# A two-block transformer kernel in fp32: the first gate and up weights of the feed-forward multiplied directly instead of through quarter sums

## The chip, the cores and the metric

The kernel runs on one core of a Trainium2 chip. The metric is device time in microseconds (us) of one execution. The core has a matrix engine (TensorE, PE in the profile), a vector engine (VectorE, DVE), an activation engine (ScalarE, ACT), GpSimd (POOL) and a queue for DMA issues (SyncE, SP). They run their own programs in order and wait for each other through semaphores. Matmul results land in PSUM, which has 8 banks of 512 fp32 columns.

## What is computed

Two transformer blocks over 512 tokens of width 1024. The first has two kinds of attention and a mixture of 64 experts; the second has retention and latent attention, and then the part that matters here:

```
h = h + rmsnorm(mix, post_mix_norm)
hn = rmsnorm(h, pre_ffn_norm)
ff = (silu(hn @ w_gate) * (hn @ w_up)) @ w_down        # D_FF = 2816
h = h + rmsnorm(ff, post_ffn_norm)
```

A gated embedding of each layer follows. All of it is fp32.

## The kernel before

**Three products for one.** A product of fp32 matrices in full precision is made from parts: each operand is split into a high part (rounded by a copy of ACT, `act_split`, `hi_until`) and a low part (operand minus high part, a subtraction on DVE, `dve_split`, `lo_until`), and `three` (L666 to L670) multiplies high by high, low by high and high by low into the same bank. A weight unit of 128 x 2048 elements is loaded by SP into one of three raw buffers (`whole`), turned into a high part in one of two buffers (`high`) and a low part (`low`). Before ACT writes the high part of unit k, `hi_until` calls `used(act, order[k - PARTS])`, which waits until PE has filled the last bank that unit k-2 feeds. From the first gate unit on, the high parts lie in buffers of their own (`late_hi`), the low parts in `late_lo`, the raw weights in `late_raw`.

**Gate and up by seven products.** The 22 units of gate and up (11 each, taken in turn: gate 0, up 0, gate 1, ...) are each a 1024 x 256 block of weights. It is cut into quarters A11, A12, A21, A22, the turned rows hn into quarters B11 to B22, and the product is made from seven products of quarters or of sums of quarters (Winograd's form of Strassen's method) instead of eight. For that GpSimd makes the sums S1 to S4 of each unit in place (`quarter_sums`, L2894 to L2902), ACT the high parts (`sums_hi`, L792), DVE the low parts (`sums_lo`, L799), and the results are added up again by DVE when they leave PSUM (`first_sums` to `last_sums`, L1643 to L1678). Each unit takes 7 x 4 x 3 = 84 matmuls of 256 columns. On the side of the rows the sums T1 to T4 are made once:

```
PRODUCTS = (("A11", "B11"), ("A12", "B21")), (("S1", "T1"), ("S2", "T2")), (("S4", "B22"), ("A22", "T4")), (("S3", "T3"),)
```

**The stretch before it.** The output projection of the mixer ("om", L668 to L670 with the tile omT) makes four tiles of 128 tokens, each in two banks, 12 matmuls of 512 columns for a bank: tile i goes to banks 2i (om0) and 2i+1 (om1), so that bank 6 is the last of unit om0 and bank 7 the last of om1. DVE then takes tile by tile: it adds the banks (L1584), multiplies by the gain (L1586), waits for ACT's sum of squares (L654) and its root (L658), adds the scaled rows to x (L1588), and, one tile later, scales x by the root of the next norm into `xn6` (L1577). PE turns the rows of xn6 by transposes into banks (L1314).

In the kernel before, GpSimd makes the quarter sums of three units and then the low parts of the first two in that stretch (L799 on POOL, four operations), and ACT makes their high parts between the norms (`between_norms`). The transposes go to banks so that one holds two chunks of half the tokens; the quarters are read straight from the banks, by ACT for high parts (L807) and for plain copies of the other half (L1895), by DVE for low parts (L1605) and differences (L1612). The first unit's products are queued in PE behind each of these in turn: B11, B21, T1, T2, B22, T4, T3. All of the queues' orders are written out by hand.

Behind gate and up comes w_down ("down"), whose left operands are the products ff in high and low parts.

Of the kernel before, what the change touches and what calls it, by code (L numbers as in the profile page):

```python
# [20 lines left out]
F32 = mybir.dt.float32  # L21
# [154 lines left out]
def build(nc, a, out):  # L176
    ctx = ExitStack()
    with ctx:
# [9 lines left out]
        def at(name, lo, shape, dt=F32):  # L188
# [28 lines left out]
        OPS = ("B11", "B21", "T1", "T2", "B22", "T4", "T3")  # L217
        OPS_AT = (8192, 16384, 10240, 38656, 40704, 42752, 44800)
        op_hi = {n: at(n + "h", F0 + lo, [4, Q], F32R) for n, lo in zip(OPS, OPS_AT)}
        op_lo, op_raw = [{n: at(n + k, F0 + lo + 1024, [4, Q], d) for n, lo in zip(OPS, OPS_AT)}  # L220
                         for k, d in (("l", F32R), ("r", F32))]
# [6 lines left out]

        copies, partial = at("copies", F0 + 35328, [2, Q]), at("partial", F0 + 35840, [3, Q])
        up_sum = at("up_sum", F0 + 36608, [4, Q])  # L230
# [165 lines left out]

        ff_units = [units_of[name][n] for n in range(n_ff) for name in ("gate", "up")]
        n_late = ff_units[0].n
        for m, u in enumerate(ff_units):
            u.sums = m  # L400
# [128 lines left out]
        plan("hT4", DC)  # L529

        for m, u in enumerate(ff_units):
            u.pairs = [bk.take(1, (J["hT4"][(4 * (m + 1) + k) % 8].bank,))[0] for k in range(4)]
            u.last = u.pairs[-1]
# [253 lines left out]
        def sums_hi(act, m, k):  # L787
            u = ff_units[m]
            act.wait_ge(S("w_sums"), m + 1)
            if m >= 2:  # L790
                full(act, ff_units[m - 2].last)
            act.activation(high(u, 7 * Q2)[:, SUM_PIECES[k]], whole(u, 7 * Q2)[:, SUM_PIECES[k]],  # L792
                           ACT.Copy).then_inc(S("sums_hi"), 1)

        def sums_lo(eng, m, k):
            u = ff_units[m]
# [368 lines left out]
        OP_ORDER = ("B11",) * 4 + ("B21",) * 4 + ("T1", "T2", "B22", "T4", "T3")  # L1165

        def op_ready(name, c):

            first = OP_ORDER.index(name) + 1
            return first + c if OP_ORDER.count(name) == 4 else first  # L1170

        def rows_half(c, h):

            job = J["hT4"][4 * h + c // 2]
            return banks[job.bank][:, Q * (c % 2):Q * (c % 2 + 1)], job
# [5 lines left out]
        def pe_second(pe):  # L1181
# [121 lines left out]
            def half_rows(j, i, c):  # L1303

                lo = Q * (c % 2) + P * (i % 2)
                return banks[J["hT4"][j].bank][:, lo:lo + P]

            for job in J["hT4"]:
                claim(pe, job)
            for i in range(NT):  # L1310
                pe.wait_ge(S("xn6"), i + 1)
                for c in range(DC):
                    j = 4 * (i // 2) + c // 2
                    mm = pe.transpose(half_rows(j, i, c), xn6(i)[:, P * c:P * (c + 1)], ident)  # L1314
                    if i % 2 and c % 2:
                        fill(mm, J["hT4"][j])
# [3 lines left out]
            for m, u in enumerate(ff_units):  # L1320
                his, los = quarters(high(u, 7 * Q2)), quarters(low(u, 7 * Q2))
                for k, job in enumerate(u.pairs):
# [4 lines left out]
                    for h, (left, right) in enumerate(PRODUCTS[k]):  # L1327
                        for c in range(4):
                            if m == 0:
                                pe.wait_ge(S("op_lo"), op_ready(right, c))  # L1330
                            mm = three(pe, banks[job.bank][:, Q * h:Q * (h + 1)], (his[left][:, c, :], los[left][:, c, :]),
                                       (op_hi[right][:, c, :], op_lo[right][:, c, :]), c == 0, c == 3)
# [134 lines left out]
        def dve_second(v, chain, evac):  # L1467
# [131 lines left out]
            def direct_lo(name, first):  # L1599
                for c in range(4):  # L1600
                    src, job = rows_half(first + c, 0)
                    full(v, job)

                    v.wait_ge(split_hi, hi_number["op", name, c | 1])
                    v.scalar_tensor_tensor(op_lo[name][:, c, :], src, PRM("pre_ffn", first + c),  # L1605
                                           op_hi[name][:, c, :].bitcast(F32), ALU.mult, ALU.subtract).then_inc(S("op_lo"), 1)

            def less(name, first, other, signal):

                for c in range(4):  # L1610
                    src, job = rows_half(first + c, 0)
                    ins = v.scalar_tensor_tensor(op_raw[name][:, c, :], src, PRM("pre_ffn", first + c), other[:, c, :],  # L1612
                                                 ALU.mult, ALU.subtract)
                    if c % 2:
                        free(ins, job)
                read(v, [job])
                v.sem_inc(S("op_sums"), 1)

            direct_lo("B11", 0)
            v.wait_ge(split_hi, hi_number["op", "b12"])  # L1620
            less("T1", 0, op_raw["T3"], 1)
            direct_lo("B21", 4)
            v.wait_ge(split_hi, hi_number["op", "b22"])
            chain(v.tensor_tensor(op_raw["T2"][:, :, :], op_raw["B22"][:, :, :], op_raw["T1"][:, :, :], ALU.add))
            v.sem_inc(S("op_sums"), 1)
            operand_lo("T1")
            less("T4", 4, op_raw["T2"], 3)
# [4 lines left out]
            operand_lo("T3")  # L1632

# [30 lines left out]
            def middle_sums(m):  # L1664
# [3 lines left out]
                if m:  # L1668
                    read(v, [ff_units[m - 1].pairs[3]])
# [1281 lines left out]
```

## Time and profile before

| what | value |
|---|---|
| median of 3 runs | 2074.44 us (2073.94 to 2077.29) |
| profiled execution, its own time | 2073.24 us |
| its span | 2071.4 us |
| busy in the span: PE, DVE, ACT, POOL | 86%, 44%, 36%, 15% |
| mean granted TensorE clock | 0.954 of full speed |

The span is what the profiler sees from the first to the last instruction; 1.8 us of the execution lie around it. Times below are us from the span's start. PE's clock has two levels, 1.2 and 2.4 GHz, shown as 0.5 and 1.0 of full speed. In a timeline a row's duration runs until its result is there; operations of one engine follow each other about 0.1 us before that.

### The profile page before, as it was taken

To read this page: it belongs to the slowest core of one execution; us is meant where nothing else is said; L and a number is where in the kernel's file an instruction comes from. 1 tells how busy PE (TensorE), PEld (TensorE's weight loads), DVE (VectorE), ACT (ScalarE), POOL (GpSimd) and SP (SyncE) were. 2 spreads that over 40 slices of the span, in tenths; PEclk is the share of its full clock that TensorE was granted. 3 is DMA by queue.
4 is the path that set the end of the run, shared out by engine and by line. 5 is a ranking of instruction groups with operands and counts; after the bars stand their busy time and mean duration, and the time that the engine had idled before them with its cause. 6 is when DMAs were issued, how large, how long until landed. Compare 5 with 4: busy or idle time off the path is not lost.

```text
span 2071.4 us, 37813 instructions
## 1 busy us (share of the span) xinstructions
PE 1772.4 (86%) x15166; PEld 1280.3 (62%) x15166; DVE 918.5 (44%) x1703; ACT 740.2 (36%) x1369; POOL 313.1 (15%) x298
## 2 busy tenths in 40 slices
PE   7999999787877787767777877789999599999988
PEld 5677788544444443434444444378767499998876
DVE  4455435532222222222222222365375878886245
ACT  4444522233222322232223222343465544444143
POOL 0000000000000000000000000640011668870020
PEclk9999999899999999999999999999999799999999
DMA  6222222699999999999999999843232033334212
GB/s 206 77 83 63 81 102 97 281 371 420 428 425 428 426 426 425 428 425 426 426 426 426 427 425 426 356 124 92 65 92 67 5 103 103 103 102 143 102 61 81
DMA packets 108338, 506.17 MB, mean 244 GB/s; under 512 B 9400, under 2 KB 58808, under 8 KB 74976
## 3 DMA queue, kind: packets, MB, share of 16 engines
q1 hardware_dynamic: 100144, 491.28, 59.4%
q10 hardware_dynamic: 6512, 9.73, 1.7%
q0 software_dynamic: 1600, 4.02, 0.7%
q8 instruction: 58, 0.95, 0.2%
q14 instruction: 24, 0.20, 0.0%
HBM read 497.32 MB, written 2.11 MB: 241 GB/s over the span
## 4 chain that ended last, share of the span: by engine, by line
PE 59%; DMA 29%; DVE 7%; issue 2%; ACT 2%; SPq 1%; POOL 0%; ACTq 0%; POOLq 0%; DVEq 0%
DMA ring<-in_w 27%; PE bank L668 13%; PE bank L669 12%; PE bank L670 12%; PE bank L2477 8%; PE bank L2389 4%; PE bank L2468 3%; PE bank L856 2%; PE bank L882 1%; PE bank L868 1%; DMA raw<-in_w_in 1%; SPq L2027 1%; PE bank L2486 1%; PE bank L1204 1%; DVE x L1588 0%
## 5 line engine op out<-in xcount | busy, mean ns | idle before, releaser
L2477 PE MATMUL bank<-ring,XTs 128*32 128x256 f32 x4032 | 284.8, 426 | 112.6 <-DMA ring<-in_w 109.7
L2730 DVE TENSOR_TENSOR x<-x,bank 128x512 f32<-128x512 f32 x264 | 163.9, 682 | 482.7 <-PE bank L2468 481.9
L2477 PEld LDWEIGHTS bank<-ring,XTs 128*32 128x32 f32 x4032 | 154.2, 120 | 245.0 <-issue 181.5
L2486 PE MATMUL bank<-ring,aT 128*32 128x256 f32 x2048 | 123.8, 381 | 90.0 <-DVE aT L2750 90.0
L2256 ACT ACTIVATE y<-bank 32x256 f32<-32x256 f32 x256 | 96.1, 376 | 225.1 <-PE bank L2468 139.0
L668 PE MATMUL bank<-hTh,w_hi 128*128 128x512 f32 x362 | 147.2, 407 | 5.5 <-DVE hTl L820 2.9
L2389 PE MATMUL bank<-arena,oh 128*32 128x256 f32 x2048 | 144.2, 421 | 4.4 <-DVE oh L2712 2.9
L772 DVE TENSOR_TENSOR w_lo<-raw,w_hi 128x2048 fp32r<-128x2048 f32 (+4 forms) x47 | 98.2, 2094 | 110.8 <-ACT w_hi L756 110.7
L2486 PEld LDWEIGHTS bank<-ring,aT 128*32 128x32 f32 x2048 | 66.7, 109 | 128.5 <-issue 96.2
L670 PE MATMUL bank<-hTl,w_hi 128*128 128x512 f32 x362 | 143.1, 395 | 0.0
L669 PE MATMUL bank<-hTh,w_lo 128*128 128x512 f32 x362 | 143.0, 395 | 0.0
L2836 POOL COPY sel<-side 128x8 f32 x62 | 11.9, 191 | 866.9 <-DVE og L2720 866.9
L2468 PE MATMUL bank<-y,g 64*128 64x512 f32 x528 | 131.4, 615 | 2.8 <-ACT y L2256 1.8
L2389 PEld LDWEIGHTS bank<-arena,oh 128*32 128x32 f32 x2048 | 90.1, 124 | 56.1 <-DVE oh L2712 18.3
L2225 ACT ACTIVATE xe<-bank 128x256 f32<-128x256 f32 x64 | 24.6, 384 | 276.1 <-PE bank L2389 276.1
L799 DVE TENSOR_TENSOR late_lo<-late_raw,late_hi 128x2048 fp32r<-128x2048 f32 (+1 forms) x40 | 95.7, 2393 | 17.6 <-ACT late_hi L792 17.6
L756 ACT ACTIVATE w_hi<-raw 128x2048 fp32r<-128x2048 f32 (+4 forms) x47 | 80.3, 1718 | 63.3 <-PE bank L670 61.7
L2228 ACT ACTIVATE XTs<-bank 128x256 f32<-128x256 f32 x64 | 24.7, 386 | 171.4 <-PE bank L2395 171.4
L668 PEld LDWEIGHTS bank<-hTh,w_hi 128*128 128x128 f32 x362 | 68.7, 190 | 27.1 <-issue 8.2
L2468 PEld LDWEIGHTS bank<-y,g 64*128 64x128 f32 x528 | 45.4, 186 | 61.9 <-issue 59.2
L2744 DVE COPY Hs<-bank 128x256 f32<-128x256 f32 x64 | 27.2, 425 | 125.0 <-PE bank L2477 125.0
L668 PE MATMUL bank<-w_hi,hTh 128*128 128x512 f32 (+2 forms) x232 | 80.2, 346 | 2.6 <-ACT arena L1831 2.2
(479 smaller groups left out, 3862.7 us busy)
## 6 DMA issues: line engine op xcount, KB each, us to landing
ring<-in_w SPq DMA_DIRECT2D x190, 2048.0 KB, 19.6
raw<-in_w_in SPq DMA_DIRECT2D x25, 1024.0 KB, 5.4
late_raw<-in_w_gate SPq DMA_DIRECT2D x11, 1024.0 KB, 5.4
late_raw<-in_w_up SPq DMA_DIRECT2D x11, 1024.0 KB, 5.4
late_raw<-in_w_down SPq DMA_DIRECT2D x11, 1024.0 KB, 5.0
raw<-in_w_out SPq DMA_DIRECT2D x4, 1024.0 KB, 5.0
third<-in_w SPq DMA_DIRECT2D x2, 2048.0 KB, 22.6
raw<-in_w_o SPq DMA_DIRECT2D x4, 1024.0 KB, 5.6
```

The costliest lines, as they stand in the source:

```text
L668: pe.matmul(dst, left[0], right[0], start=start, stop=False)
L669: pe.matmul(dst, left[1], right[0], start=False, stop=False)
L670: return pe.matmul(dst, left[0], right[1], start=False, stop=stop)
L756: ins = act.activation(hi, src, ACT.Copy)
L772: ins = v.tensor_tensor(lo, src, hi, ALU.subtract)
L799: eng.tensor_tensor(low(u, 7 * Q2)[:, cols], whole(u, 7 * Q2)[:, cols], high(u, 7 * Q2)[:, cols].bitcast(F32), ALU.subtract).then_inc(S("s ...
L2256: act.activation(y2[to:to + BLK, Q * (j % 2):Q * (j % 2 + 1)], Yb[BLK * j:BLK * (j + 1), :], ACT.Copy).then_inc(y_out, 1)
L2389: mm = pe.matmul(Xp[BLK * j:BLK * (j + 1), :], oh[u][:, t, :], h2[:, t, Q * j:Q * (j + 1)], start=(t == 0), stop=(t == NT - 1))
L2468: mm = pe.matmul(Sb[t % 2][n][:, :], g2[rows_, P * t:P * (t + 1)], y2[rows_, :], start=True, stop=True)
L2477: mm = pe.matmul(Hb[BLK * j:BLK * (j + 1), :], XTs[u][:, 4 * (c % 2) + 2 * h + c // 2, :], w[:, at_:at_ + Q], start=(h == 0 and c == 0), s ...
L2486: mm = pe.matmul(Yb[BLK * j:BLK * (j + 1), :], aT[:, r, h, :], ring[3 * u + 2][:, at_:at_ + Q], start=(h == 0 and r == 0), stop=(h == 1 an ...
L2730: ins = v.tensor_tensor(xs, xs, Sb[t % 2][n][:, :], ALU.add)
```

## The change

Gate 0 and up 0 no longer go through quarter sums: each is multiplied directly, two banks of 8 chunks x 3 = 24 matmuls of 512 columns, over the whole rows (high part `hTh`, low part `hT4l`). The list of units with quarter sums is now `sum_units`, the other 20. The transposes fill one bank per chunk with all 512 tokens. ACT copies each bank once to SBUF (`turned4`) with the gain of the norm, and makes the high part from that copy; DVE makes the low part from it as well. The quarters B11, B21 and B22 are read out of these; T1 to T4 are made by DVE from `turned4` behind the low parts. GpSimd only makes quarter sums, of the third unit on; the low parts of the sums are DVE's. ACT's high parts of gate 0 and up 0 are made by `hi_until`, that of gate 0 ahead of the norms' loop, that of up 0 behind the first root. DVE makes the low parts of gate 0 and up 0 (`lo_until`) behind the eight low parts of the rows. The core of the diff:

```diff
+        sum_units = ff_units[2:]
...
+        J["gate"], J["up"] = bk.take(2), bk.take(2)
+        for u, name in zip(ff_units, ("gate", "up")):
+            u.last = J[name][-1]
+
+        for u in sum_units:
+            u.pairs = bk.take(4)
...
         def sums_hi(act, m, k):
-            u = ff_units[m]
+            u = sum_units[m]
             act.wait_ge(S("w_sums"), m + 1)
-            if m >= 2:
-                full(act, ff_units[m - 2].last)
+            used(act, order[u.n - PARTS])
...
+            pe_to_feature(pe, J["hT4"], lambda i, c: xn6(i)[:, P * c:P * (c + 1)], lambda i: pe.wait_ge(S("xn6"), i + 1))
+            for name, u in zip(("gate", "up"), ff_units):
+                loaded(pe, u)
+                wh, wl = parts(u)
+                for job in J[name]:
+                    claim(pe, job)
+
+                for c in range(DC):
+                    if name == "gate":
+                        pe.wait_ge(S("op_lo"), c + 1)
+                    for k, job in enumerate(J[name]):
+                        cols = slice(P * k, P * (k + 1))
+                        mm = three(pe, banks[job.bank][:, :], (wh[:, c, cols], wl[:, c, cols]), (hTh[:, c, :], hT4l[:, c, :]),
+                                   c == 0, c == DC - 1)
...
+            for c in range(DC):
+                v.wait_ge(split_hi, hi_number["hT4", c])
+                v.tensor_tensor(halves_of(hT4l[:, c, :]), turned_chunk(c), halves_of(hTh[:, c, :].bitcast(F32)),
+                                ALU.subtract).then_inc(S("op_lo"), 1)
+            lo_until(v, ff_units[1].n)
+            v.wait_ge(S("op_lo"), DC)
+            b11, b12, b21, b22 = op_raw["T1"], op_raw["T3"], op_raw["T4"], op_raw["T2"]
+            for dst, one, other, op in ((b11, b11, b12, ALU.subtract), (b12, b22, b12, ALU.subtract), (b22, b22, b11, ALU.add),
+                                        (b21, b21, b22, ALU.subtract)):
+                chain(v.tensor_tensor(dst[:, :, :], one[:, :, :], other[:, :, :], op))
                 v.sem_inc(S("op_sums"), 1)
...
             operand_lo("T1")
             operand_lo("T2")
-            v.wait_ge(S("op_third"), 1)
-            operand_lo("B22")
+            sums_lo(v, 0, 0)
+            sums_lo(v, 0, 1)
             operand_lo("T4")
             operand_lo("T3")
+            for f, job in enumerate(J["up"]):
+                full(v, job)
+                v.wait_ge(S("silu_there"), f + 1)
+                ins = v.tensor_tensor(ff(f), ff(f), banks[job.bank][:, :], ALU.mult)
...
-            between_norms = (lambda: (sums_hi(act, 0, 0), sums_hi(act, 0, 1)), lambda: sums_hi(act, 1, 0),
-                             lambda: sums_hi(act, 1, 1), lambda: None)
+            hi_until(act, ff_units[0].n)
             for i in range(NT):
                 read(act, [J["om0"][i], J["om1"][i]])
                 n5.act(act, i, mixo[:, i, :], xn6(i), ssq, rstd)
                 if i:
                     act.wait_ge(S("x3"), i)
                     n6.act(act, i - 1, x[:, i - 1, :], xn6(i - 1), ssq2, rstd2)
-                between_norms[i]()
+                else:
+                    hi_until(act, ff_units[1].n)
...
+            for c, job in enumerate(J["hT4"]):
+                full(act, job)
+                free(act.activation(turned_chunk(c), halves_of(banks[job.bank][:, :]), ACT.Copy, scale=PRM("pre_ffn", c)), job)
+                if c:
+                    turned_hi(c - 1)
+            turned_hi(DC - 1)
...
-            for m in range(3):
-                quarter_sums(m)
-            for m in range(2):
-                for k in range(2):
-                    sums_lo(pool, m, k)
...
+            act.wait_ge(S("ff"), FC)
             for f in range(2, FC):
                 product_hi(f)
```

**Where instructions moved.** ACT's queue at the norms before, from the issue of the gain's load. `filledN` is the semaphore by which PE says that bank N is full, `arrivedN` says that a load has landed, `freedN` that a bank was read; L654 is the sum of squares, L658 the root:

```order
L2095 DMA gain_mix<-in_post_mix_norm 128x1024 [waits freed5,freed4]
L654 ACTIVATE xn6s,small<-arena 128x1024 [waits freed1,freed0]
L658 ACT_TABLE_LOAD
L658 ACTIVATE small<-small 128x1 [waits tile_means]
L792 ACTIVATE late_hi<-late_raw 128x2048 [waits w_sums]
L792 ACTIVATE late_hi<-late_raw 128x1536 [waits w_sums]
L654 ACTIVATE xn6s,small<-arena 128x1024 [waits freed3,freed2]
```

The same place in the changed kernel, whose line numbers are some 7 higher (L763 is `hi_until`, L661 the squares, L665 the root):

```order
L2089 DMA gain_mix<-in_post_mix_norm 128x1024 [waits freed5,freed4]
L763 ACTIVATE late_hi<-late_raw 128x2048 [waits filled6,arrived2]
L661 ACTIVATE xn6s,small<-arena 128x1024 [waits freed1,freed0]
L665 ACT_TABLE_LOAD
L665 ACTIVATE small<-small 128x1 [waits tile_means]
L763 ACTIVATE late_hi<-late_raw 128x2048 [waits filled7,arrived0]
L661 ACTIVATE xn6s,small<-arena 128x1024 [waits freed3,freed2]
```

The high part of gate 0 now stands ahead of the first sum of squares and waits for bank 6; that of up 0 stands behind the first root and waits for bank 7.

DVE's queue in the changed kernel, from the last xn6 (L1588 there) to the low parts of the first unit with sums (L805):

```order
L1588 TENSOR_SCALAR xn6s<-x,small 128x1024 [waits dve_own]
L1612 TENSOR_TENSOR hT4l<-turned_75,hTh 128x512 [waits split_hi] x4
L1612 TENSOR_TENSOR hT4l<-turned_76,hTh 128x512 [waits split_hi] x4
L779 TENSOR_TENSOR late_lo<-late_raw,late_hi 128x2048 [waits hi_made] x2
L1619 TENSOR_TENSOR turned_75<-turned_75 128x1024 [waits op_lo]
L1619 TENSOR_TENSOR turned_75<-turned_76,turned_75 128x1024 [waits dve_own]
L1619 TENSOR_TENSOR turned_76<-turned_76,turned_75 128x1024 [waits dve_own]
L1619 TENSOR_TENSOR turned_76<-turned_76 128x1024 [waits dve_own]
L1607 TENSOR_TENSOR T1l<-turned_75,T1h 128x1024 [waits dve_own,split_hi]
L1607 TENSOR_TENSOR T2l<-turned_76,T2h 128x1024 [waits split_hi]
L805 TENSOR_TENSOR late_lo<-late_raw,late_hi 128x2048 [waits sums_hi]
```

The low part of gate 0, which PE's first direct product waits for (`loaded`), stands behind all eight low parts of the rows; the quarter sums of the rows stand behind both.

## Rows read from the trace of the kernel before

**Rows 1.** Page, the chain that ended last, shares by engine.
```profile
PE 59%; DMA 29%; DVE 7%; issue 2%; ACT 2%; SPq 1%; POOL 0%; ACTq 0%; POOLq 0%; DVEq 0%
```
**Rows 2.** Windows: length; busy PE, PEld, DVE, ACT, POOL; clock, DMA share, GB/s.
```profile
1602.90:1618.70 15.80, 15.80 (x68) 12.34 (x66) 13.72 (x18) 10.61 (x14) 15.41 (x10) 1.00 0.22 72
1618.70:1642.40 23.70, 5.00 (x24) 4.62 (x24) 21.92 (x20) 8.34 (x19) 19.94 (x5) 0.58 0.00 0
...
1644.40:1662.30 17.90, 13.41 (x87) 12.73 (x86) 15.79 (x23) 11.00 (x19) 2.37 (x1) 0.84 0.00 1
1662.30:1874.30 212.00, 211.80 (x1765) 211.60 (x1764) 177.05 (x231) 91.07 (x107) 163.48 (x76) 1.00 0.33 105
```
**Rows 3.** Timeline of PE: start, duration, operation, idle before and its releaser.
```profile
1615.52 0.39 PE L670 MATMUL bank<-w_lo,omT 128*128 128x512 f32 x1
1641.06 3.67 PE L1314 MATMUL bank<-cst,xn6s 128*128 128x128 f32 x16 [6.08 <-DVE xn6s L1577]
1644.43 0.55 PE L668 MATMUL bank<-B11h,late_hi 128*128 128x256 f32 x1
1662.29 0.28 PE L668 MATMUL bank<-B11h,late_hi 128*128 128x256 f32 x1
1874.43 0.40 PE L668 MATMUL bank<-late_hi,ffh 128*128 128x512 f32 x1
1874.66 0.40 PE L669 MATMUL bank<-late_hi,ffl 128*128 128x512 f32 x1
```
**Rows 4.** Timeline of DVE in the norms.
```profile
1602.96 1.28 DVE L1584 TENSOR_TENSOR arena<-mix_scaled,bank 128x512 f32<-128x512 f32 x2 [4.17 <-DMA gain_mix<-in_post_mix_norm]
1607.24 2.23 DVE L1588 SCALAR_TENSOR_TENSOR x<-mix_scaled,small,x 128x1024 f32<-128x1024 f32 x1
1621.27 4.79 DVE L1588 SCALAR_TENSOR_TENSOR x<-mix_scaled,small,x 128x1024 f32<-128x1024 f32 x1
1631.19 4.16 DVE L1586 TENSOR_TENSOR mix_scaled<-arena,gain_mix 128x1024 f32<-128x1024 f32 x1
1636.01 3.71 DVE L1588 SCALAR_TENSOR_TENSOR x<-mix_scaled,small,x 128x1024 f32<-128x1024 f32 x1
1640.25 0.75 DVE L1577 TENSOR_SCALAR xn6s<-x,small 128x1024 f32<-128x1024 f32 x1
1641.71 0.75 DVE L1577 TENSOR_SCALAR xn6s<-x,small 128x1024 f32<-128x1024 f32 x1
```
**Rows 5.** Timeline of POOL there.
```profile
1604.73 2.27 POOL L2899 TENSOR_TENSOR late_raw<-late_raw 128x512 f32<-128x512 f32 x1
1619.48 19.16 POOL L799 TENSOR_TENSOR late_lo<-late_raw,late_hi 128x2048 fp32r<-128x2048 f32 x4
```
**Rows 6.** Timeline of ACT at the first norm.
```profile
1604.34 1.06 ACT L654 ACTIVATE xn6s<-arena 128x1024 f32<-128x1024 f32 x1 [7.88 <-DVE arena L1584]
```
**Rows 7.** Groups by form: count, busy us, mean ns, idle before.
```profile
L1741 DVE SCALAR_TENSOR_TENSOR e_tok<-e_tok,small,gain_ple 128x1024 f32<-128x1024 f32 x4 | 4.9, 1278 | 0.0
L1596 DVE TENSOR_TENSOR T4l<-T4r,T4h 128x1024 fp32r<-128x1024 f32 x1 | 1.2, 1219 | 0.0
L756 ACT ACTIVATE late_hi<-late_raw 128x2048 fp32r<-128x2048 f32 x16 | 30.6, 1914 | 95.8 <-PE bank L670 95.8
L807 ACT ACTIVATE hTh<-bank,small 128x512 fp32r<-128x512 f32 x8 | 4.7, 703 | 0.7 <-PE bank L636 0.7
L772 DVE TENSOR_TENSOR late_lo<-late_raw,late_hi 128x2048 fp32r<-128x2048 f32 x16 | 36.6, 2291 | 81.2 <-ACT late_hi L756 81.2
```
**Rows 8.** Timeline of ACT and of DVE behind gate and up.
```profile
1876.53 4.79 ACT L807 ACTIVATE ffh<-ffr 128x512 fp32r<-128x512 f32 x9
...
1878.87 12.13 DVE L819 TENSOR_TENSOR ffl<-ffr,ffh 128x512 fp32r<-128x512 f32 x20
```
**Rows 9.** Windows after PE idled until 1653.31: same columns as rows 2.
```profile
1655.00:1656.50 1.50, 1.48 (x7) 1.19 (x6) 1.50 (x2) 1.50 (x2) 0.00 (x0) 0.50 0.00 0
1656.50:1657.00 0.50, 0.50 (x4) 0.50 (x4) 0.50 (x1) 0.50 (x2) 0.00 (x0) 0.71 0.00 0
```

More of the change, by code:

```diff
@@ L1163, in build, with turned_chunk, halves_of @@
         NX = 2 * NBLK
[L1165 to L1175, printed above, removed]
+        OP_ORDER = ("T1", "T2", "T4", "T3")
+        def turned_chunk(c):
+            return turned4[c // 4][:, :, c % 4, :]
+        def halves_of(t):
+            return t.rearrange("p (h n) -> p h n", h=2)
         def sums_of(job):
@@ L1302, in pe_second, with operand @@
                     fill(mm, job)
[L1303 to L1311, printed above, removed]
-                for c in range(DC):
[L1313 to L1316, printed above, removed]
+            pe_to_feature(pe, J["hT4"], lambda i, c: xn6(i)[:, P * c:P * (c + 1)], lambda i: pe.wait_ge(S("xn6"), i + 1))
[4 more added lines that the diff above has]
+                    claim(pe, job)
+                for c in range(DC):
+                    if name == "gate":
[4 more added lines that the diff above has]
+                                   c == 0, c == DC - 1)
+                        if c == DC - 1:
+                            fill(mm, job)
+            def operand(name, c):
+                if name in op_hi:
+                    return op_hi[name][:, c, :], op_lo[name][:, c, :]
+                first, cols = dict(B11=(0, slice(0, Q)), B21=(4, slice(0, Q)), B22=(4, slice(Q, T)))[name]
+                return hTh[:, first + c, cols], hT4l[:, first + c, cols]
             PRODUCTS = (("A11", "B11"), ("A12", "B21")), (("S1", "T1"), ("S2", "T2")), (("S4", "B22"), ("A22", "T4")), (("S3", "T3"),)
-            for m, u in enumerate(ff_units):
+            for m, u in enumerate(sum_units):
                 his, los = quarters(high(u, 7 * Q2)), quarters(low(u, 7 * Q2))
@@ L1608, in less @@
[L1608 to L1616, printed above, removed]
-                v.sem_inc(S("op_sums"), 1)
-            direct_lo("B11", 0)
@@ L1668, in middle_sums @@
                 if m:
-                    read(v, [ff_units[m - 1].pairs[3]])
-                chain(v.tensor_tensor(u2, copies[:, m % 2, :], sixth, ALU.add))
+                    read(v, [sum_units[m - 1].pairs[3]])
+                chain(v.tensor_tensor(u2, copies[m % 2], sixth, ALU.add))
                 free(v.tensor_tensor(u4, u2, fifth, ALU.subtract), job)
             def second_sums(m):
-                job = ff_units[m].pairs[2]
-                read(v, ff_units[m].pairs[1:2])
+                job = sum_units[m].pairs[2]
+                read(v, sum_units[m].pairs[1:2])
                 full(v, job)
@@ L1916, in product_hi @@
                 act_split(act, ("ff", f), ff_hi(f), ff(f))
-            direct_hi("B11", 0)
-            other_half("b12", op_raw["T3"], 0)
-            direct_hi("B21", 4)
-            other_half("b22", op_raw["B22"], 4)
-            operand_hi("T1", 1)
-            operand_hi("B22", 1)
-            operand_hi("T2", 2)
-            operand_hi("T4", 3)
-            act.wait_ge(S("op_third"), 1)
-            operand_hi("T3", 3)
-            for m, u in enumerate(ff_units):
-                n, ready = m // 2, 1 <= m < len(ff_units) - 1
+            for f, job in enumerate(J["gate"]):
+                full(act, job)
+                free(act.activation(ff(f), banks[job.bank][:, :], ACT.Silu), job)
+                read(act, [job])
+                act.sem_inc(S("silu_there"), 1)
+            operand_hi("T1", 1)
+            operand_hi("T2", 3)
+            sums_hi(act, 0, 0)
+            sums_hi(act, 0, 1)
+            operand_hi("T4", 4)
+            operand_hi("T3", 2)
+            for m, u in enumerate(sum_units):
+                n, ready = m // 2 + 1, m < len(sum_units) - 1
                 if m % 2:
                     for k in (2, 3):
-                        gated(n, k, ff_units[m - 1].pairs[3])
+                        gated(n, k, sum_units[m - 1].pairs[3])
                 full(act, u.pairs[0])
-                act.activation(copies[:, m % 2, :], sums_of(u.pairs[0])[0], ACT.Copy).then_inc(S("copied"), 1)
+                act.activation(copies[m % 2], sums_of(u.pairs[0])[0], ACT.Copy).then_inc(S("copied"), 1)
                 if ready:
```

103 lines of the change are left out of this document (37 added, 66 removed).

## The prediction

> **What bounds the kernel now.** I read the page's chain first: 59% of the span is PE and 29% DMA [rows 1]. The DMA share is the experts' weights, which the change leaves alone. It works between the mixer's output projection and w_down, so I cut that stretch into windows. The reader is to see four things. Until 1618.7 PE is fully busy with the projection [rows 2]. From 1618.7 to 1642.4 PE is busy for 5.0 of 23.7 us while DVE is busy for 21.9: the norms on DVE are the bound. The first unit of gate and up, 1644.43 to 1662.29, takes 17.9 us, with PE busy for 13.4 and its clock at 0.84. The other 21 units take 212.1 us, 10.10 each, with PE never idle [rows 2, 3]. So what counts is the moment at which w_down's first matmul starts, 1874.43. What comes later moves as a whole.
>
> The norms are slow for a reason. DVE's scaled add L1588 takes 4.79 and 3.71 us for two tiles and the multiply L1586 takes 4.16 [rows 4], where the same forms elsewhere take 1.28 and 1.22 [rows 7]. GpSimd works for 19.2 us without a break beside them [rows 5], and once it has stopped the xn6 operations take 0.75.
>
> **1. The norms.** The first tile's adds wait for the gain's load and end at 1604.2; ACT's squares start at 1604.34 [rows 4, 6]. In the change ACT's queue has the high part of gate 0 ahead of these squares, and it waits for bank 6, the last bank of om0. PE's last matmul into that bank starts at 1615.52 and ends at 1615.9 [rows 3]. The copy takes 1.9 us [rows 7], 1.8 until the next can start, so the squares start at about 1617.8, 13.5 us late. All of DVE's norm chain is queued behind the first root. PE is not: its four tiles have banks of their own. From squares to L1588 the rows give 1607.24 - 1604.34 = 2.90 us, a table load among it [rows 4, 6], so L1588 of the first tile starts at 1620.7. The copy for up 0 behind the first root hides beside DVE: bank 7 is full at 1618.7, and ACT is free again at 1622.3, before the next adds end at 1623.3.
>
> From there on GpSimd is silent. It still has the sums of the third unit, whose load is over by 1606.4 (a DMA share of 0.22 in 15.8 us [rows 2]); four operations of at most the 2.27 of [rows 5] are over by 1615.5, while DVE waits anyway. So DVE runs at its own pace: L1588 1.28, L1586 1.22, adds 1.28, xn6 0.75 [rows 4, 7], 0.6 for the small operations and ACT's root ahead of each scaling (1640.25 + 1.46 = 1641.71 is one xn6 and its preparation). The second tile follows after 1.28 + 1.28 + 1.22 + 0.62 = 4.4, the third and fourth after 4.4 + 0.61 + 0.75 = 5.76 each, and from the last L1588 to the end of the last xn6 it is 1.28 + 2.74 = 4.0 (2.74 from 1639.72, the end of L1588, to 1642.46). Sum 19.9: the last xn6 ends at 1640.7, against 1642.46 now. **Gain 1.8.** Nearly all that the quiet GpSimd gives back is spent on the wait for bank 6.
>
> **2. From the last xn6 to the first product.** Now 1644.43 - 1642.46 = 2.0 us. In the change PE turns the third tile's eight chunks from 1639.2 on and the fourth's behind them, at 0.23 each [rows 3]; the first bank is full, and ACT starts, at 1641.35. ACT then has 16 operations: eight scaled copies out of banks, 4.7 us from the first start to the last end [rows 7], and eight high parts, 8/9 of 4.79 [rows 8]; together 9.0. DVE keeps up (0.61 each [rows 8]) and ends the eighth low part 0.7 later. Only then comes the low part of gate 0, 2.29 [rows 7], for which PE waits. With 0.2 for hand-overs PE starts at 1653.5, 12.8 us behind the last xn6. **Loss 10.8.** PE's waits chunk by chunk hide nothing, since the weights' low part comes last.
>
> The Trainium skill says (ScalarE: Activation LUTs, What ACT_TABLE_LOAD costs) that a per-partition pointer operand costs an activation about 93 ns; by its figure the copies would follow each other every 0.61 us and the sum would be 0.2 us higher. The rows' eight copies with such a scale decide, and I keep their 4.7.
>
> **3. The first two units.** Now 1644.43 to 1662.29 and 10.10 more: 28.0 us. In the change 2 x 48 = 96 matmuls of 512 columns at 0.23 [rows 3] make 22.1. The clock is at half when PE starts, as it was after the idle time before 1653.31, and there it took until about 1656.7, 3.4 us, to come back (0.71 in the half microsecond from 1656.5 [rows 9]); that loses half of 3.4. Sum 23.8. **Gain 4.2.** Had PE gone on with seven products it would be 20.2; the two extra eighths cost less than the first unit's waits for B21, T1 and T2 that they remove.
>
> **4. What hides behind them.** PE needs T1, T2 and the third unit's parts at 1653.5 + 23.8 = 1677.3. DVE makes the second low part and the four sums of quarters by 1661 (2.3 + 4 x 1.25). ACT is in PE's way here: its two silus wait for gate's banks, full at 1666.2, so that T1's high part starts at 1667.4, T2's ends at 1669.5, the third unit's two pieces at 1671.3 and 1672.7. DVE's low parts follow at 1673.6 to 1674.6 and 1676.6, 3 us and 4 us ahead of their need (the second piece is wanted at 1680.2). GpSimd's next sums run from about 1671.6, since their load starts when gate's banks are full. Cost 0. Cover gone, it is the rival below.
>
> **5. The rest.** 20 units at 10.10 make 202.0. ACT's new wait for all products ahead of w_down's high parts costs at most the 2 us until DVE's last one; PE has 11 us of w_down's first part to do meanwhile. 0.
>
> **Sum.** -1.8 + 10.8 - 4.2 = +4.8: w_down starts at 1653.5 + 23.8 + 202.0 = 1879.3 instead of 1874.43. The profiled execution took 2073.24 and would take 2078.1; its median is 1.2 higher, which gives 2079.2. I say **2079**, slower by 0.2%. About 0.2%, 4.1 us, is what a measurement of this kernel can tell from no change, and I am close to it.
>
> **Rivals.**
> *The wait for bank 6 costs nothing (faster).* It would have to be over by 1602.4, so that the copy is done when the squares are due: if bank 6 counted as full by an earlier use. The queue's row names bank 6, and PE fills it for om0 only at 1615.9; against it. Then L1588 starts at 1607.24 as now, the chain runs its 19.9, about 1 more for the sums of the third unit beside the first tile, and the last xn6 ends at 1628.2, 14.2 earlier: 2079.2 - 12.4 = 2066.8. Chance 0.07.
> *GpSimd is not what stretches DVE.* Then the chain from the first L1588 keeps its 35.2 us instead of 19.9, and the time is 2094.5. The return to 0.75 when GpSimd stops speaks against. 0.03.
> *The first unit with sums waits.* DVE's two low parts, T4, T3 and the two multiplies of up have GpSimd beside them. If they stretch as L1588 does, the next unit's low part, wanted at 1687.4, comes 1 to 3 us late: 2080.2 to 2082.2. By the Trainium skill (SBUF — State Buffer, Who interferes with whom) a DVE operation with two SBUF inputs and a GpSimd one that reads SBUF exclude each other for a whole instruction; four sums of 1.3 would then add at most 5.2 to that queue, which is within this rival. The steady units, which hold as many of both and never make PE wait [rows 2], speak against. 0.15.
> *The start is shorter than worked out.* ACT and DVE hand over faster, the clock comes up during the transposes, or the loop of norms overlaps more: 1 to 3 us less, 2076 to 2078. 0.15.
> *The change doesn't do what it says* holds in part: GpSimd does work between the norms, on one unit, but DVE waits then; it is in the forecast.
>
> **How the numbers follow.** Forecast 0.60, 2077 to 2081.5. Slower by over 0.2% is above 2078.6: 0.42 of the forecast's 0.60, with 0.15 and 0.03, 0.60. Within 0.2%: 0.18 + 0.15 = 0.33. Faster: 0.07. The range of 8 in 10 takes in the two small rivals beside the forecast, with 2 us for the estimates added up: 2074.5 to 2083.5.
>
> **What would show it.** Right: ACT idle until about 1616 ahead of the high part of gate 0; L1588 at 1.28 for all four tiles; PE idle for about 10 us behind the transposes, released by DVE's low part of gate 0; first direct product near 1653.5; 20 units of 10.1. Wrong: ACT's squares near 1604, L1588 still above 3 us, or PE waiting behind up 0.

## The result, and the profile after

The changed kernel takes 2079.02 us (median of 20 runs, 2075.02 to 2086.2), the kernel before on the same chip 2074.55 (20 runs, 2071.45 to 2079.13): a ratio of 1.0021, 95% interval 1.0013 to 1.0029. It is slower by 0.2%, as forecast, to 0.02 us of the forecast time. So close a hit says little: the 20 runs lie 11 us apart, and the interval of the ratio alone is 3.3 us wide. Whether the terms are right is read below.

The page's shares of the changed kernel, beside [rows 1]:

```profile
span 2077.9 us, 37612 instructions
...
PE 59%; DMA 29%; DVE 6%; ACT 2%; issue 2%; SPq 1%; POOL 1%; ACTq 0%; POOLq 0%; DVEq 0%
```

The shares cannot show a change of this size. The stretch cut into windows by stage does, as in [rows 2]; columns: length, then busy time and count of PE, weight loads, DVE, ACT and GpSimd, PE's granted clock, DMA share, GB/s:

```profile
1602.90:1615.90 13.00, 13.00 (x58) 10.46 (x57) 2.51 (x3) 0.00 (x0) 5.12 (x4) 1.00 0.54 180
1615.90:1640.40 24.50, 8.27 (x37) 6.78 (x36) 14.73 (x27) 13.39 (x22) 0.00 (x0) 0.70 0.00 0
1640.40:1653.50 13.10, 5.20 (x24) 4.40 (x22) 7.35 (x14) 10.51 (x22) 0.00 (x0) 0.63 0.00 0
1653.50:1677.30 23.80, 20.49 (x84) 16.82 (x85) 15.84 (x12) 9.78 (x10) 2.26 (x1) 0.86 0.14 45
1677.30:1879.00 201.70, 201.37 (x1664) 200.46 (x1663) 171.78 (x215) 86.39 (x102) 162.36 (x76) 1.00 0.34 105
```

In the first window ACT does nothing and DVE 2.51 us of work in 13: both wait, DVE for the gain's load until 1606.39 and then for ACT. GpSimd's four operations all fall into that wait. In the last window PE is full again.

DVE's timeline in the norms of the changed kernel, the answer to [rows 4]; columns: start, duration, engine, line, operation, out<-in, count, and the idle time before with what ended it:

```profile
1606.39 1.28 DVE L1595 TENSOR_TENSOR arena<-mix_scaled,bank 128x512 f32<-128x512 f32 x2 [4.25 <-DMA gain_mix<-in_post_mix_norm]
1607.78 1.23 DVE L1597 TENSOR_TENSOR mix_scaled<-arena,gain_mix 128x1024 f32<-128x1024 f32 x1
1622.41 0.15 DVE L669 TENSOR_SCALAR small<-small 128x1 f32<-128x1 f32 x1 [13.40 <-ACT xn6s L661]
1623.85 0.16 DVE L671 RECIPROCAL small<-small 128x1 f32<-128x1 f32 x1 [1.29 <-ACT small L665]
1624.05 1.28 DVE L1599 SCALAR_TENSOR_TENSOR x<-mix_scaled,small,x 128x1024 f32<-128x1024 f32 x1
...
1643.29 0.75 DVE L1588 TENSOR_SCALAR xn6s<-x,small 128x1024 f32<-128x1024 f32 x1
```

All four scaled adds, as a group (count, then busy us and mean ns):

```profile
L1599 DVE SCALAR_TENSOR_TENSOR x<-mix_scaled,small,x 128x1024 f32<-128x1024 f32 x4 | 5.1, 1285 | 0.1
```

ACT's timeline, the answer to [rows 6]:

```profile
1619.35 1.92 ACT L763 ACTIVATE late_hi<-late_raw 128x2048 fp32r<-128x2048 f32 x1 [19.54 <-PE bank L677]
1621.17 1.04 ACT L661 ACTIVATE xn6s<-arena 128x1024 f32<-128x1024 f32 x1
```

And PE's timeline, the answer to [rows 3]:

```profile
1642.64 3.68 PE L643 MATMUL bank<-cst,xn6s 128*128 128x128 f32 x16 [0.71 <-DVE xn6s L1588]
1656.81 0.79 PE L675 MATMUL bank<-hTh,late_hi 128*128 128x512 f32 x1 [10.49 <-DVE late_lo L779]
1657.40 0.63 PE L676 MATMUL bank<-hTh,late_lo 128*128 128x512 f32 x1
...
1882.61 0.40 PE L675 MATMUL bank<-late_hi,ffh 128*128 128x512 f32 x1
```

The wait for bank 6 ends ACT's 19.54 us of idle time ahead of gate 0's high part (with the copy behind it, ACT's squares start 13.4 us later behind the adds than in experiment 1), and the queue's end is the 10.49 us for which PE waits on DVE's low part of gate 0. PE starts on the units and finds its clock at half (0.63 us a matmul instead of 0.39).

**One shift to take out first.** The norms' first adds start at 1606.39, in the kernel before at 1602.96 [rows 4]: 3.4 us late before any changed instruction. Two windows of both executions tell why; first the kernel before, then the changed one:

```profile
1500.00:1530.00 30.00, 26.57 (x122) 19.75 (x114) 27.80 (x37) 20.78 (x31) 8.99 (x18) 1.00 0.46 124
1530.00:1560.00 30.00, 28.74 (x167) 21.02 (x167) 17.69 (x63) 17.98 (x55) 0.00 (x0) 1.00 0.11 36
```

```profile
1500.00:1530.00 30.00, 27.60 (x119) 20.18 (x118) 26.31 (x35) 20.01 (x31) 8.99 (x18) 0.95 0.47 125
1530.00:1560.00 30.00, 27.70 (x146) 19.97 (x146) 17.07 (x55) 16.93 (x46) 0.00 (x0) 0.94 0.11 37
```

The granted clock was 0.95 and 0.94 there instead of 1.00, and 5% and 6% of 30 us are 3.3 us. It goes with the execution and not with the change: in the first experiment's, whose code there is the same, the clock is 1.00 in both windows and the adds start at 1602.68, while experiments 2 and 5 again had 0.94 in both and start them at 1605.46 and 1605.32. The clock is not all of it: experiment 3 had 1.00 in both windows and its adds start at 1606.01, for a reason that lies further ahead and was not looked into. On the other side, PE's last stretch from w_down's first matmul to the end of the span took 197.0 us before and 195.3 after; over the nine profiled executions it was 195.3 twice, 197.0 five times, 199.7 and 199.8, and went with the kernel's content in no way that I can see. So traces are compared below by four marks, counted from the first adds: that takes both shifts out.

| kernel | adds to the end of the last xn6 | to the first product | to w_down's first matmul | adds to w_down | median us, ratio |
|---|---|---|---|---|---|
| before | 39.50 | 1.97 | 230.00 | 271.47 | 2074.55, 1 |
| the change | 37.65 | 12.77 | 225.80 | 276.22 | 2079.02, 1.0021 |
| 1. no wait for bank 6 | 26.31 | 12.37 | 225.83 | 264.51 | 2069.07, 0.9971 |
| 2. low part first | 37.77 | 3.47 | 225.23 | 266.47 | 2069.62, 0.9970 |
| 3. both | 26.24 | 3.47 | 225.69 | 255.40 | 2059.44, 0.9918 |
| 4. before, its low parts on DVE | 28.19 | 4.41 | 228.78 | 261.38 | 2064.18, 0.9946 |
| 5. as 3, GpSimd busy | 34.64 | 3.08 | 224.09 | 261.81 | 2067.58, 0.9950 |
| 6. as 3, sums after the norms | 24.26 | 4.03 | 225.05 | 253.34 | 2058.41, 0.9916 |
| 7. as 3, GpSimd copies | 28.72 | 3.08 | 225.86 | 257.66 | 2060.47, 0.9927 |

Each mark is a start read from a timeline; the end of the last xn6 is its start and 0.75. The ratios are against runs of the kernel before made beside each kernel (medians 2074.13 for experiments 1 to 4 and 2075.12 for 5 to 7). They are not the quotients of the medians and differ from these by up to 0.0014, 3 us; the intervals given below are wider than that. The change adds 4.75 us between the adds and w_down.

### The profile page after: what moved, and what is told of

The parts are those of the page before. It is cut to its first block, busy times and chain, and to the rows that moved or that the text cites. A ratio compares the mean times of both kernels' runs of the same rounds, so it can differ in the third digit from the quotient of the medians.

```text
span 2077.9 us, 37612 instructions
## 1 busy us (share of the span) xinstructions
PE 1771.9 (85%) x15094; PEld 1274.1 (61%) x15094; DVE 902.7 (43%) x1683; ACT 737.9 (36%) x1362; POOL 278.6 (13%) x285
## 4 chain that ended last, share of the span: by engine, by line
PE 59%; DMA 29%; DVE 6%; ACT 2%; issue 2%; SPq 1%; POOL 1%; ACTq 0%; POOLq 0%; DVEq 0%
DMA ring<-in_w 27%; PE bank L675 13%; PE bank L676 12%; PE bank L677 12%; PE bank L2471 8%; PE bank L2383 4%; PE bank L2462 3%; PE bank L862 2%; PE bank L888 1%; PE bank L874 1%; DMA raw<-in_w_in 1%; SPq L2021 1%; PE bank L2480 1%; DVE w_lo L779 1%; PE bank L1207 1%
## 5 line engine op out<-in xcount | busy, mean ns | idle before, releaser
L805 DVE TENSOR_TENSOR late_lo<-late_raw,late_hi 128x2048 fp32r<-128x2048 f32 (+1 forms) x40 | 97.0, 2427 | 15.8 <-ACT late_hi L798 15.8
L763 ACT ACTIVATE w_hi<-raw 128x2048 fp32r<-128x2048 f32 (+4 forms) x47 | 80.3, 1718 | 64.1 <-PE bank L677 62.6
L675 PE MATMUL bank<-hTh,late_hi 128*128 128x256 f32 (+1 forms) x272 | 81.4, 299 | 10.8 <-DVE late_lo L779 10.5
```

Of the source, the lines that this page charges most:

```text
L675: pe.matmul(dst, left[0], right[0], start=start, stop=False)
L763: ins = act.activation(hi, src, ACT.Copy)
L805: eng.tensor_tensor(low(u, 7 * Q2)[:, cols], whole(u, 7 * Q2)[:, cols], high(u, 7 * Q2)[:, cols].bitcast(F32), ALU.subtract).then_inc(S("s ...
```

## Experiments

My theory was the forecast's: the change quiets GpSimd and that is worth 12 to 14 us, but it puts ACT's first squares behind a wait for bank 6 (13.5 us) and the low part of gate 0 behind eight low parts of rows (10 us). The rivals: GpSimd is not what stretches DVE, and the wait or the queue order costs nothing because something else is late too. Experiments 1 and 2 take one price each away.

### 1. Gate 0's and up 0's high parts without the wait

Line 760, in the function that makes high parts on ACT. Nobody reads the buffers of these two units' high parts before, so the wait that was taken from the general case can go:

```diff
-                if k >= PARTS:
+                if k >= PARTS and u.late not in (0, 1):
```

> The changed kernel, but ACT's high parts of gate 0 and up 0 do not wait for om's last banks (their buffers are not the ones that om reads). My theory: that wait holds all four norms back by 13.5 us, so the first L1588 (L1599 there) starts about 4.3 us behind the first adds, the last xn6 ends 12.4 us earlier against the adds, and the time falls by 12.4 us against the changed kernel, to about 2066.6 (before: 2074.5). Rival 1, the banks' wait is hidden by something else that is late too (the gain's load, PE's transposes): no change, 2079. Rival 2, GpSimd's sums of the third unit now meet the norms and stretch DVE again: 2070 to 2074.

Measured: 2069.07 us (12 runs), ratio 0.9971, interval 0.9959 to 0.9983. DVE's timeline, with the gap behind the first L1597 gone:

```profile
1602.68 1.28 DVE L1595 TENSOR_TENSOR arena<-mix_scaled,bank 128x512 f32<-128x512 f32 x2 [4.08 <-DMA gain_mix<-in_post_mix_norm]
1604.07 1.23 DVE L1597 TENSOR_TENSOR mix_scaled<-arena,gain_mix 128x1024 f32<-128x1024 f32 x1
...
1606.95 2.08 DVE L1599 SCALAR_TENSOR_TENSOR x<-mix_scaled,small,x 128x1024 f32<-128x1024 f32 x1
1608.95 1.27 DVE L1595 TENSOR_TENSOR arena<-mix_scaled,bank 128x512 f32<-128x512 f32 x2
1610.33 2.19 DVE L1597 TENSOR_TENSOR mix_scaled<-arena,gain_mix 128x1024 f32<-128x1024 f32 x1
```

The wait for bank 6 is real and it is the whole delay: without it the scaled add comes 4.3 us behind the adds, and adds to xn6 falls by 11.3. From adds to w_down it is 11.7, between the medians 10.0: the median lies just below the 2070 to 2074 of rival 2, and that rival holds in part. I had expected 13.5 less 1 us for GpSimd's sums of the third unit; those sums now run beside the first two tiles and cost 2 (experiment 6). PE still waits 11.2 us for the low part of gate 0.

### 2. The low part of gate 0 ahead of the rows' low parts

One line in DVE's order, ahead of the loop over the eight chunks:

```diff
+            lo_until(v, ff_units[0].n)
             for c in range(DC):
                 v.wait_ge(split_hi, hi_number["hT4", c])
```

> The changed kernel, but DVE makes the low part of gate 0 ahead of the eight low parts of the rows instead of behind them, in the 2.6 us in which it waits for ACT's first high part. My theory: PE's first direct product starts with the first chunk, about 3.4 us behind the start of ACT's copies instead of 12, and goes on at half clock and then as ACT delivers a chunk each 1.09 us; it needs 12.7 us for gate, so gate ends about 9.4 us earlier: 2069.6. Rival 1, only the 2.3 us of the low part itself are won: 2076.7. Rival 2, PE starts earlier but the third unit's parts become late, since ACT makes them behind the silus: between the two.

Measured: 2069.62 us (12 runs), ratio 0.9970, interval 0.9957 to 0.9983. DVE and then PE:

```profile
1643.15 2.28 DVE L779 TENSOR_TENSOR late_lo<-late_raw,late_hi 128x2048 fp32r<-128x2048 f32 x1
1645.86 0.69 DVE L1613 TENSOR_TENSOR hT4l<-turned,hTh 128x512 fp32r<-128x512 f32 x1 [0.43 <-ACT hTh L813]
```

```profile
1646.70 0.47 PE L675 MATMUL bank<-hTh,late_hi 128*128 128x512 f32 x1 [1.20 <-DVE hT4l L1613]
```

The low part lies where DVE waited for ACT's first high part anyway, and PE starts 3.47 us behind the last xn6 instead of 12.77. It then takes the chunks as they come, each 1.10 apart while six matmuls (two banks) take 1.4 at full clock, so it never waits for one. Of the 9.75 us between the adds and w_down 9.30 are the earlier start. My expectation had half clock here too; in this execution the clock was full from the first product on, so the first two units took 21.85 us and no longer 23.36, and most of that was lost again in the other 20, which took 203.38 and not 202.44.

### 3. Both

> Both edits together (no wait for om's last banks, low part of gate 0 first). My theory: the two are in series on the path and add up: -12.4 and -9.4 give about 2057.2 against 2079.0, and 17 us less than before the change. Rival: one hides the other, and the time is that of the better one alone, 2066 to 2070.

Measured: 2059.44 us (6 runs), ratio 0.9918, interval 0.9897 to 0.9938. Between adds and w_down the two edits give 11.71 and 9.75 alone and 20.82 together, 0.64 less than the sum: the two prices lie one after the other on the path and all but add up. The median is 2.2 us above the expected 2057.2. **This kernel is faster than both, by 0.8% than the one before** (0.7% by the medians).

### 4. The kernel before, with GpSimd's four low parts on DVE

Nothing else of the change. The two calls for unit 0 go behind the last xn6 on DVE, the two for unit 1 behind the rows' first low parts, and GpSimd's are taken out:

```diff
+            sums_lo(v, 0, 0)
+            sums_lo(v, 0, 1)
...
+            sums_lo(v, 1, 0)
+            sums_lo(v, 1, 1)
...
-            for m in range(2):
-                for k in range(2):
-                    sums_lo(pool, m, k)
```

> The kernel before, but the low parts of the first two units' sums are made by DVE (unit 0 behind the last xn6, unit 1 behind T3), and GpSimd makes quarter sums alone. This is the quiet GpSimd by itself, with nothing else of the change. My theory: GpSimd's 19.2 us stretched DVE's operations; without them the last xn6 ends about 12.4 us earlier, PE's first product starts 4 us later behind it, net -8.4: 2066.1. Rival, GpSimd's work is not what stretched DVE: the norms stay as long and the time rises by the 4 us, to 2078.5.

Measured: 2064.18 us (6 runs), ratio 0.9946, interval 0.9927 to 0.9965, 2 us better than expected. DVE's timeline, to be held against 2.23, 4.79 and 3.71 for L1588 in [rows 4]:

```profile
1608.07 2.33 DVE L1588 SCALAR_TENSOR_TENSOR x<-mix_scaled,small,x 128x1024 f32<-128x1024 f32 x1
...
1614.67 1.58 DVE L1588 SCALAR_TENSOR_TENSOR x<-mix_scaled,small,x 128x1024 f32<-128x1024 f32 x1
...
1622.20 1.28 DVE L1588 SCALAR_TENSOR_TENSOR x<-mix_scaled,small,x 128x1024 f32<-128x1024 f32 x1
...
1627.95 1.29 DVE L1588 SCALAR_TENSOR_TENSOR x<-mix_scaled,small,x 128x1024 f32<-128x1024 f32 x1
1631.90 3.95 DVE L799 TENSOR_TENSOR late_lo<-late_raw,late_hi 128x2048 fp32r<-128x2048 f32 x2
```

The norms shorten by 11.3 us and the low parts, 19.16 on GpSimd [rows 5], cost DVE 3.95 for unit 0. The first product comes 2.4 us later behind the last xn6 (4 expected), and the stretch from there to w_down is 1.2 shorter. GpSimd still makes the sums of three units here, so the first tiles keep some of their length (2.33 and 1.58). So GpSimd without its low parts was worth some 10 us to the kernel before by itself, and the rest of the change, as it was made, cost 15. With both edits the rest of the change is a gain: experiment 3 is 6.0 us shorter than this kernel from adds to w_down, 2.0 in the norms, 0.9 up to the first product and 3.1 behind it.

### 5 and 7. GpSimd's load put back

Is it GpSimd at all, or something that went with it? The kernel of experiment 3 gets four operations on GpSimd ahead of the third unit's sums; they read that unit's raw weights and write an area that nothing reads, so nothing of the computation changes. In 5 they are subtractions (two inputs), in 7 copies (one):

```diff
+            u = sum_units[0]
+            pool.wait_ge(arrived[u.n % RAW], u.loads)
+            for k in range(4):
+                n = (UNIT, 7 * Q2 - UNIT)[k % 2]
+                chain(pool.tensor_tensor(idle_area[:, 0:n], whole(u, n), whole(u, n), ALU.subtract))
```

In 7 the last line is `chain(pool.tensor_copy(idle_area[:, 0:n], whole(u, n)))`.

> The kernel of the third experiment (no wait for bank 6, low part of gate 0 first; 2059.4 us) with GpSimd's work put back beside the norms: four subtractions of 2048 and 1536 columns from the third unit's raw weights into an idle area, which nothing reads, ahead of the sums of its quarters. They take about as long as the four low parts did in the kernel before (19.2 us). Theory (GpSimd's reads and writes are what stretches DVE's operations of the norms): DVE's L1599, L1597 and xn6 go from 1.3-2.3 us to 2-5 us, the last xn6 comes 8 to 14 us later behind the first adds, and the time is 2059.4 + 11 = 2070 (2067 to 2074). Rival (what stretched DVE in the kernel before was its other data, the late_lo and late_hi area or ACT's high parts at the same time): DVE keeps its 1.3-2.3, time 2059 to 2062. Second rival (only the instruction count of GpSimd matters, and the sums of the quarters come too late for the third unit): PE waits behind up 0 and not before gate 0.

> As the kernel with GpSimd's work put back, but with four copies (one input) of the same columns instead of four subtractions (two inputs). Theory A (any GpSimd operation on SBUF stretches DVE's): DVE's operations of the norms that run beside a copy take 2 us and more, and the time lies above 2059.4 by about as much as GpSimd is busy longer, in the ratio of the subtractions' run. Theory B (it takes GpSimd's two inputs from SBUF): DVE keeps 1.2 to 1.3 beside the copies, and only the sums of quarters stretch it: 2059 to 2061.

Measured: 5 takes 2067.58 us (6 runs), ratio 0.9950, interval 0.9933 to 0.9968; 7 takes 2060.47 us (6 runs), ratio 0.9927, interval 0.9910 to 0.9944. GpSimd's timeline of 5, then of 7:

```profile
1609.26 15.52 POOL L2904 TENSOR_TENSOR idle_area<-late_raw 128x2048 f32<-128x2048 f32 x4 [81.08 <-DMA late_raw<-in_w_gate]
```

```profile
1605.89 9.67 POOL L2904 COPY idle_area<-late_raw 128x2048 f32<-128x2048 f32 x4 [77.97 <-DMA late_raw<-in_w_gate]
```

DVE's groups in the norms (busy us and mean ns after the bar), 5 and then 7:

```profile
L1600 DVE SCALAR_TENSOR_TENSOR x<-mix_scaled,small,x 128x1024 f32<-128x1024 f32 x4 | 11.1, 2767 | 0.1
L1598 DVE TENSOR_TENSOR mix_scaled<-arena,gain_mix 128x1024 f32<-128x1024 f32 x4 | 7.1, 1772 | 0.4
L1589 DVE TENSOR_SCALAR xn6s<-x,small 128x1024 f32<-128x1024 f32 x4 | 5.3, 1316 | 0.1
L1596 DVE TENSOR_TENSOR arena<-mix_scaled,bank 128x512 f32<-128x512 f32 x8 | 5.1, 676 | 4.2 <-DMA gain_mix<-in_post_mix_norm 4.2
```

```profile
L1600 DVE SCALAR_TENSOR_TENSOR x<-mix_scaled,small,x 128x1024 f32<-128x1024 f32 x4 | 7.6, 1889 | 0.1
L1598 DVE TENSOR_TENSOR mix_scaled<-arena,gain_mix 128x1024 f32<-128x1024 f32 x4 | 6.0, 1492 | 0.4
```

The theory stands: the work alone brings the stretched operations back. With nothing beside them (experiment 6) the norms take 24.26 us; 22.7 us of subtractions and sums make them 34.64, and 16.9 us of copies and sums 28.72. Take off the 1.98 that the sums cost in experiment 3 (as if they cost the same here), and 15.52 us of subtractions cost about 8.4 and 9.67 us of copies about 2.5. So theory B of experiment 7 is wrong, a copy stretches DVE's operation too (L1600 took 2.55 and 2.17 us beside them), but it costs 0.26 us for each of its microseconds where a subtraction costs 0.54.

That a copy costs less need not have to do with its one input. Single instructions of GpSimd, each beside the DVE operation that it met, from the timelines of both engines, first in 5:

```profile
1609.26 3.60 POOL L2904 TENSOR_TENSOR idle_area<-late_raw 128x2048 f32<-128x2048 f32 x1 [81.08 <-DMA late_raw<-in_w_gate]
1609.60 4.34 DVE L1600 SCALAR_TENSOR_TENSOR x<-mix_scaled,small,x 128x1024 f32<-128x1024 f32 x1
```

and then in 7:

```profile
1605.89 1.91 POOL L2904 COPY idle_area<-late_raw 128x2048 f32<-128x2048 f32 x1 [77.97 <-DMA late_raw<-in_w_gate]
1606.32 2.55 DVE L1600 SCALAR_TENSOR_TENSOR x<-mix_scaled,small,x 128x1024 f32<-128x1024 f32 x1
...
1610.17 1.23 DVE L1598 TENSOR_TENSOR mix_scaled<-arena,gain_mix 128x1024 f32<-128x1024 f32 x1
1610.26 2.90 POOL L2904 COPY idle_area<-late_raw 128x2048 f32<-128x2048 f32 x1
```

The subtraction ends at 1612.86 and DVE's add, begun inside it, 1.08 us later; the copy ends at 1607.80 and the add begun inside it 1.07 later. In the third pair DVE began 0.09 us first: it kept its 1.23, and the copy took 2.90 instead of 1.91. The long operations of the kernel before do the same: 4.79, 4.16 and 3.71 all end 1.08 or 1.09 us behind the end of one of GpSimd's low parts (1624.97, 1634.27, 1638.64). So both kinds of instruction hold DVE up in the same way, until they are over, and the copy is over sooner (1.91 us for 2048 columns against 3.60). Instructions of one length with one and with two inputs were not compared, so that the inputs count for nothing beyond this is not shown.

In time, 7 cannot be told from 3; the reading rests on the trace. Experiment 5 lost 6.6 us against 3 by the ratios, 8.1 by the medians and 6.4 from adds to w_down; PE had its full clock when gate 0 started, which gave back 1.6 (last section).

### 6. GpSimd's sums held back until the norms are over

```diff
+            pool.wait_ge(S("xn6"), NT)
             for m in range(len(sum_units)):
                 quarter_sums(m)
```

> The kernel of the third experiment with GpSimd's sums of quarters held back until the last xn6 is written, so that GpSimd does nothing at all between the norms. Theory (the 2 us by which the first two experiments' norms fell short of the chain worked out at 19.9 us from the first scaled add are these four sums beside DVE): L1597 and L1599 of the first two tiles go back to 1.22-1.28, the last xn6 comes 2 us earlier behind the first adds, and the time is 2057.4 (2056.4 to 2058.4), since the sums are needed only some 10 us later, when PE has two units of 22 us to do. Rival (the sums, now beside DVE's low parts of the rows and of up 0, stretch those instead): the first product comes no earlier, 2059 to 2061.

Measured: 2058.41 us (6 runs), ratio 0.9916, interval 0.9897 to 0.9936. Its groups of DVE in the norms:

```profile
L1599 DVE SCALAR_TENSOR_TENSOR x<-mix_scaled,small,x 128x1024 f32<-128x1024 f32 x4 | 5.1, 1285 | 0.1
...
L1597 DVE TENSOR_TENSOR mix_scaled<-arena,gain_mix 128x1024 f32<-128x1024 f32 x4 | 4.9, 1226 | 0.4
```

The norms lose their last 1.98 us, as the theory said, and 0.56 is lost again between the last xn6 and the first product (the rival's half: the sums now stretch DVE's low part of the first chunk to 1.64 us from 0.69, and the first GpSimd sum itself takes 3.24 us instead of 1.29). The ratio is that of experiment 3, so whether the rest, 1.4 us, shows in the time stays open.

## Why the prediction was right

**The norms.** Forecast 37.7 from adds to the last xn6 (1640.7 - 1602.96), measured 37.65. L1588 of before is L1599 of after, and all four take 1.28. The chain that I worked out for an undisturbed DVE, 4.3 and 19.9 us, is what experiment 6 runs: 24.26. Gain forecast 1.8, measured 1.85.

**From the last xn6 to the first product.** Forecast 12.8, measured 12.77: ACT starts 0.82 us behind the last xn6 (0.65 worked out), 16 operations of ACT from 1644.86 to 1653.74 are 8.9 (9.0 worked out), and the low part of gate 0 is the release of PE. The copies out of banks with a scale per partition:

```profile
1644.86 1.27 ACT L1889 ACTIVATE turned<-bank,prm 128x512 f32<-128x512 f32 x2 [1.80 <-PE bank L643]
...
1652.55 1.19 ACT L813 ACTIVATE hTh<-turned 128x512 fp32r<-128x512 f32 x2
```

A copy and a high part take 1.09 together in the steady part. An estimate by the Trainium skill's figure (ScalarE: Activation LUTs, What ACT_TABLE_LOAD costs) would have been 0.2 us higher; by the trace it came out at the rows'.

**The first two units.** Forecast 23.8, measured 23.36: first product 1656.81, first unit with sums 1680.17. PE's matmuls take 0.63 us until 1659.5 and 0.39 from 1659.96 on, so the clock came back after 3.1 us and not 3.4; the forecast was 0.44 too long, and this is 0.15 of it; 0.2 more is that the 96 matmuls follow each other at a little less than the rounded 0.23 (21.85 us for all of them at full clock in experiment 2). From the first product to w_down it is 225.80 against 230.00, a gain of 4.20 for 4.2 forecast, but two misses of 0.4 cancel in it: the first two units went from 27.94 to 23.36, a gain of 4.58, and the other 20, forecast to stay as they were, from 202.06 to 202.44. Experiment 3 against 4 gives 3.1 for the same two units: with the low parts off GpSimd the first unit of the kernel before takes 16.6 us and no longer 17.9. Its waits gave that: 4.5 us of them before and 2.5 in experiment 4, while the clock took 0.7 back (0.84 granted before, 0.69 there).

**What hides.** Right in its result. DVE's T4 and T3 took 2.31 and 2.32 us beside GpSimd instead of 1.22, held up as the Trainium skill's rule said (SBUF — State Buffer, Who interferes with whom), but PE never waited for the third unit: from 1603 to 1885 only two of its waits are over 1 us, the transposes' and gate 0's, and its wait for a low part of the sums is 0.2 in all. The rival of a first unit that waits did not happen.

**The rivals.** The wait that costs nothing: against it the 19.54 us on ACT, and experiment 1. GpSimd is not the cause: against it experiments 4, 5 and 6. The time a rival gave was good too: 2066.8 for a kernel without the wait, 2069.07 measured. 1 of the missing 2.3 us is that the third unit's sums cost 2 and not the 1 allowed; the rest was not traced.

**What was lucky.** The three stretches and their sum agree within 0.1 us each, but the median of runs mixes stretches that vary (3.4 us ahead of the norms, 195.3 to 199.8 behind w_down's start). An execution could have come out 3 us off with every step right. The term for the clock was lucky too: the forecast took 1.7 us from one row of the kernel before, the change lost about 1.6, and the same products lost between nothing and 2.4 in the experiments (last section). That two misses of 0.4 cancel behind the first product is luck as well.

## To carry to other kernels

A change that quiets an engine is paid out only where that engine's victim is the bound, and only if the same edit does not put a new wait at the head of the victim's queue: write down, for each queue, what now stands ahead of the first instruction on the path, and what that waits for. Here the norms gained 13.3 us by the quiet GpSimd and lost 11.4 by the wait, the first product came 10.8 later behind them (9.3 by the order of one queue), and the direct units gave back 4.2: a loss of 4.7 us, 0.2%, which two lines turned into a win of 0.8%. A general rule's wait (every high part waits for the last user of its buffer) is worth a look where a unit moves to a place in which nobody reads the buffer before.

## What the runs showed of the hardware

- GpSimd and DVE hold each other up for the rest of an instruction (experiments 5 and 7): beside GpSimd's subtractions DVE's scaled add takes 3.7 to 4.8 us for 1.28 and the multiply 2.4 to 4.2 for 1.22 (the kernel before and experiment 5), beside copies the scaled add takes 2.2 to 2.6, and the multiply, which began just ahead of one, its 1.23. DVE's xn6, which reads one tensor from SBUF, is held up as well: 2.62 and 1.34 for 0.75. Adds with one input from a bank never stretched: 676 to 682 ns in experiments 3, 5, 6 and 7 and in the change, GpSimd busy or not. The other way round, GpSimd's sum of 512 columns takes 1.29 us alone, often 2.15 beside DVE, and up to 3.4 (experiment 2).
- The clock at which the first products run changed from execution to execution, and I can't tell what sets it: PE's granted clock was half for the first 3.1 us in the change, for 3.6 us in experiment 3 and for 5.1 us in experiment 1 (0.63 us a matmul), while in experiments 2 and 5 the first product took 0.47 and the next 0.39 to 0.40 at once. In 6 and 7 it started full and fell to half for 3.4 us in the middle of gate 0, as PE's timeline of experiment 6 has it:

```profile
1632.27 0.39 PE L677 MATMUL bank<-hT4l,late_hi 128*128 128x512 f32 x1
1632.50 0.54 PE L675 MATMUL bank<-hTh,late_hi 128*128 128x512 f32 x1
1632.83 0.63 PE L676 MATMUL bank<-hTh,late_lo 128*128 128x512 f32 x1
...
1635.82 0.49 PE L677 MATMUL bank<-hT4l,late_hi 128*128 128x512 f32 x1
```

It makes up to 2.4 us: the first two units take 21.9 us in experiments 2 and 5, 23.4 to 23.6 in the change and in 3, 6 and 7, and 24.2 in 1. The other 20 units vary as well, from 201.6 to 203.4 over these seven kernels, so the column from the first product to w_down (224.09 to 225.86) cannot be read closer than about 2 us.
